# Scores of the last head pair moved from an insertion of their own into the one before it, in two attentions of a transformer kernel

## What is computed

```python
# first block: attention by blocks (block 256, so every query sees its own block, causally)
s_own = jnp.einsum('bhqd,bhld->bhql', qb, k_own).astype(jnp.float32) * scale
s_own = jnp.where(own_pos[None, :] <= q_pos[:, None], s_own, NEG_INF)
p = jax.nn.softmax(logits, axis=-1)
out = jnp.einsum('bhql,bhld->bhqd', p_own, v_own)

# second model, first layer: attention by picked keys (top 64 by an index score, causal)
logits = jnp.einsum('bqhd,bqkhd->bhqk', qb, k_sel).astype(jnp.float32) * (dh ** -0.5)
logits = jnp.where(valid[:, None], logits, -jnp.inf)
p = jax.nn.softmax(logits, axis=-1).astype(v.dtype)
out = jnp.einsum('bhqk,bqkhd->bqhd', p, v_sel)
...
```

## Time and profile before

| | |
|---|---|
| median of 3 runs | 1026.43 us (1026.31 to 1026.63) |
| the profiled execution | 1026.1 us |
| its span, first to last instruction | 1024.3 us |
| TensorE busy | 1014.1 us (99%) |
| VectorE, ScalarE, GpSimd busy | 666.5, 568.6, 78.8 us |
| mean granted TensorE clock | 0.999 of 2.4 GHz |
| first attention beside its projection | 88.5 to 114.3 us of the span |
| second attention beside its projection | 510.4 to 537.4 us |

### The profile page before, as it was taken

The page is one execution under the profiler, slowest core; times in us unless marked ns, Lnnn a source line. Parts: engine busy times, 40 slices in busy tenths (PEclk is TensorE's granted clock), DMA queues, the critical chain, the costliest instruction groups (busy, mean ns, idle before and its releaser), DMA issues.

```text
span 1024.3 us, 14335 instructions
## 1 busy us (share of the span) xinstructions
PE 1014.1 (99%) x5178; PEld 853.1 (83%) x5178; DVE 666.5 (65%) x1077; ACT 568.6 (56%) x923; POOL 78.8 (8%) x113
## 2 busy tenths in 40 slices
PE   9999999999999999999999999999999999999997
PEld 7887888888888888787888888888899888888886
DVE  5666575467646554869957776666669858666663
ACT  6567465436545454766565654545566657454541
POOL 1010010001000000300050200000050001000000
PEclk9999999999999999999999999999999999999999
DMA  9746236314545455363424565554256324655521
GB/s 345 308 169 240 83 123 227 123 53 174 205 171 210 171 206 183 137 267 124 187 102 164 185 220 194 201 188 153 86 198 191 124 83 173 240 202 184 185 82 42
DMA packets 28959, 176.81 MB, mean 173 GB/s; under 512 B 3264, under 2 KB 3888, under 8 KB 10480
## 3 DMA queue, kind: packets, MB, share of 16 engines
q1 hardware_dynamic: 26784, 170.08, 46.0%
q0 software_dynamic: 1456, 5.48, 1.5%
q10 hardware_dynamic: 672, 0.62, 0.4%
HBM read 174.62 MB, written 1.05 MB: 172 GB/s over the span
## 4 chain that ended last, share of the span: by engine, by line
PE 94%; ACT 2%; DVE 2%; issue 1%; DMA 0%; POOL 0%; DVEq 0%; ACTq 0%; POOLq 0%
PE PS L1883 68%; PE PS L2208 10%; PE PS L2212 5%; PE PS L1957 3%; PE PS L2060 1%; ACT w_hi L646 1%; PE PS L1997 1%; PE PS L2014 1%; ACT work L826 1%; PE PS L2038 1%; PE PS L2468 1%; PE PS L2562 1%; PE PS L2571 1%; PE PS L2140 0%; DMA work<-in_gains 0%
## 5 line engine op out<-in xcount | busy, mean ns | idle before, releaser
L1883 PE MATMUL PS<-w_hi,hT 128*128 128x512 f32 (+2 forms) x1296 | 323.2, 388 | 0.6 <-DVE hT L1253 0.4
L1231 DVE SCALAR_TENSOR_TENSOR w_lo<-w_raw,gcol,w_hi 128x512 fp32r<-128x512 f32 (+4 forms) x318 | 260.7, 878 | 92.8 <-ACT w_hi L646 91.2
L646 ACT ACTIVATE w_hi<-w_raw,gcol 128x512 fp32r<-128x512 f32 (+4 forms) x326 | 244.6, 818 | 94.5 <-PE PS L1883 65.2
L1883 PEld LDWEIGHTS PS<-w_hi,hT 128*128 128x128 f32 x1296 | 236.6, 188 | 48.2 <-issue 2.6
L1225 DVE TENSOR_TENSOR w_lo<-w_raw,w_hi 128x1024 fp32r<-128x1024 f32 x118 | 143.2, 1245 | 86.9 <-ACT w_hi L646 86.1
L646 ACT ACTIVATE w_hi<-w_raw 128x1024 fp32r<-128x1024 f32 x118 | 119.6, 1052 | 97.8 <-PE PS L1883 92.6
L1883 PE MATMUL PS<-w_lo,hT 128*128 128x512 f32 (+2 forms) x648 | 172.3, 384 | 0.1
L2208 PE MATMUL PS<-hT,w_hi 128*128 128x512 f32 x448 | 156.5, 398 | 0.0
L1883 PEld LDWEIGHTS PS<-w_lo,hT 128*128 128x128 f32 x648 | 120.4, 188 | 23.9 <-DVE w_lo L1231 0.5
L2212 PE MATMUL PS<-hT,w_lo 128*128 128x256 f32 x448 | 116.6, 281 | 0.0
L1883 PE MATMUL PS<-w_hi,gT_hi 128*128 128x512 f32 x408 | 114.7, 393 | 0.0
(11 more groups left out here) (207 smaller groups left out, 821.6 us busy)
## 6 DMA issues: line engine op xcount, KB each, us to landing
w_raw<-in_w SPq DMA_DIRECT2D x64, 1024.0 KB, 4.8
w_raw<-in_w_gu SPq DMA_DIRECT2D x22, 1024.0 KB, 4.8
w_raw<-in_w_in SPq DMA_DIRECT2D x11, 1024.0 KB, 9.1
w_raw<-in_w_dn SPq DMA_DIRECT2D x22, 512.0 KB, 4.4
w_raw<-in_w_mem_k SPq DMA_DIRECT2D x4, 1024.0 KB, 4.9
w_raw<-in_w_out SPq DMA_DIRECT2D x4, 1024.0 KB, 4.8
w_raw<-in_w_cq SPq DMA_DIRECT2D x4, 1024.0 KB, 4.8
w_raw<-in_w_mem_v SPq DMA_DIRECT2D x4, 1024.0 KB, 4.8
```

Of the source, the lines that this page charges most:

```text
L646: act.activation(high, source, ACT.Copy, scale=1.0 if col is None else gcol[:, col + TURNED * k:col + TURNED * k + 1])\
L1231: ins = dve.scalar_tensor_tensor(out=lo, in0=raw, scalar=gcol[:, col + TURNED * k:col + TURNED * k + 1], in1=hi, op0=ALU.mult, op1=ALU.sub ...
L1883: mm = pe.matmul(bank(t, j)[:, 0:width], rows[:, kc0 + k, tok], w[:, s, at:at + width], start=begin and i == 0, stop=end and i == 2)
```

## The change

In both attentions the scores of pair 3 move from ahead of block (1,3) to ahead of block (0,3), right behind the turns of pair 1 (`turns_and_scores`, which was there for pairs 0 and 2). ScalarE's exponentials of pair 3 move ahead of the copy of token tile 0's projection result out of PSUM (`evict(0, ...)`), and in the first attention ahead of the split of unit 2 too, which also goes behind that copy. On VectorE the maxima of pair 3 move ahead of the split of unit 2 in the first attention; in the second one VectorE's order stays as it was. No instruction is added or removed; GpSimd's and SyncE's orders are the same.

```diff
@@ ScalarE, first attention
             for pair in range(2):
                 exponentials(moba, pair + 1)
                 copy_odd(moba, pair)
+            exponentials(moba, 3)
+            evict(0, rows2(k_tok), mem_rows)
             split_to(n["used"] + 2)
-            evict(0, rows2(k_tok), mem_rows)
-            exponentials(moba, 3)
             evict(1, rows2(k_tok), mem_rows)
@@ ScalarE, second attention
+            exponentials(dsa, 3)
             evict(0, rows2(vg_tok), even_rows)
-            exponentials(dsa, 3)
             evict(1, rows2(vg_tok), even_rows)
@@ VectorE, first attention
             copy_even(moba, 1)
+            masked_maxima(moba, 3)
             split_to(n["used"] + 2)
-            masked_maxima(moba, 3)
             copy_even(moba, 2)
@@ TensorE, first attention
-                           (0, 3): lambda: paired_turns(moba, 1), (1, 3): lambda: paired_scores(moba, 3)})
+                           (0, 3): lambda: turns_and_scores(moba, 1, 3)})
@@ TensorE, second attention
-                                                                (0, 3): lambda: paired_turns(dsa, 1), (1, 3): lambda: paired_scores(dsa, 3)})
+                                                                (0, 3): lambda: turns_and_scores(dsa, 1, 3)})
```

## The result

The changed kernel takes 1028.52 us (median of 16 runs, 1027.98 to 1030.16), the kernel before in the same series 1026.70 us (16 runs, 1026.17 to 1027.54). The difference is +1.82 us, the ratio 1.002 with a 95% interval of 1.0013 to 1.0026. So the change makes the kernel slower. The median difference is 0.18%, just under the 0.2% line, and the interval reaches from 0.13% to 0.26%, so it doesn't tell on which side of that line the loss lies.

The account below looks back on a forecast made before the run. TensorE, busy for 99% of the span, was taken to bound the kernel. Savings of 0.04 and 0.03 us and a new wait of 2.09 summed to +2.02 on 1026.43, giving 1028.45 us; range 1027.2 to 1029.2.

Parts of the forecast that it names:

- The new wait: Second attention: moved scores of pair 3 wait for VectorE's maxima 2, so TensorE stands still for 2.09 us.
- The saving: One seam between matmul kinds goes on TensorE in each attention: 0.04 us gained in the first, 0.03 in the second.
- The estimate from the Trainium skill's fixed part of a single matmul: Both attentions: some 175 ns of issue and drain saved per place, a gain of 0.35 us where the rows give 0.07.
- What the move displaces: First attention: later result copy and split of unit 2 delay the copy of turns 2; 0.8 us left, costed at nothing.
- Why VectorE is late: Second attention: two split pieces ahead of maxima 2 take 2.22 and 3.01 us, median 1.22, seemingly held by GpSimd's instructions.
- The delay absent outside the profiler: Rival, second attention: without GpSimd's delay of VectorE there is no stall, 1026.4 us; chance 0.12 for absent or halved.
- the delay fall otherwise: Same rival, second attention: GpSimd's delay differs; with half of it 1027.1 to 1027.5 us; chance 0.12 for absent or halved.
- A stall in the first attention: Rival: split of unit 2 comes too late, turns 3 wait for the copy of turns 2; 1028.9 or 1030.1 us; chance 0.04.
- A fall of the clock in the stall: Rival: TensorE granted 1.2 instead of 2.4 GHz behind the second attention's stall, each block 2.72 us more, 1031; chance 0.01.
- within 0.2%: Whole kernel: outcome that the change can't be told from no change, a line of 2.05 us; chance 0.53.

Follow-up runs that it names:

- second_only: The second attention's part of the change alone, with the first attention as in the kernel before: 1028.65 us against 1026.56, ratio 1.0023.
- before_tap_less: The kernel before with the third tap of GpSimd's convolution left out, against the kernel before: 1026.51 us against 1026.51, ratio 0.9999.

## Why the prediction was right

**The new wait: +2.09 us.** Measured 2.11 us in the changed kernel's trace, and +2.09 us for the second attention's part alone. The end of maxima 2 was foreseen as unmoved by the change, and it is: turns 1 to the end of maxima 2 is 525.21 - 522.42 = 2.79 us before and 526.00 - 523.20 = 2.80 after.

**The saving: -0.07 us.** Too small to measure in the medians, and somewhat too large in the sum. Turns 1 to turns 2 of the first attention, forecast to fall from 7.22 to 7.18 us, take 7.22, 7.22 and 7.21 in the three traces with the old order (the kernel before, second_only, before_tap_less) and 7.19 or 7.20 in the six with the new one. That is 0.02 us for 0.04. In the second attention it is 7.21 before and 7.20 in both experiments without a stall, 0.01 us for 0.03. The estimate from the Trainium skill's fixed part of a single matmul (TensorE: Matmul & The Clock Gate, section Single matmul latency), 0.35 us for both places, isn't borne out as I applied it: the joint form drops one seam and gains nearly nothing. The weight load of the scores is idle for 0.35 us behind a block and for 0.17 behind the turns, but this difference of 0.18 us doesn't come back in the distance between the starts. Why it doesn't isn't settled.

**What the move displaces: 0.** Foreseen for the first attention: the copy of turns 2 ends 0.8 us ahead of turns 3. Measured, the copy starts at 110.31 and takes 0.55, turns 3 start at 111.75, so 0.89 us:

```profile
108.03 2.36 DVE L1225 TENSOR_TENSOR w_lo<-w_raw,w_hi 128x1024 fp32r<-128x1024 f32 x2 [3.85 <-ACT w_hi L646]
110.31 0.55 DVE L1433 COPY work<-PS 128x384 f32<-128x384 f32 x1
```

VectorE idles 3.85 us ahead of the split that ScalarE now makes later, and the cover holds.

**Why VectorE is late.** The forecast read from two rows that a piece of the split is held until the GpSimd instruction beside it is over. The Trainium skill (GPSIMD Engine Reference, section Key points) names the contention, but not, in that section, its form. The runs show the form here: without the two instructions the pieces take 1.2 us, without the last one 2.21 and 1.21. The forecast passed over an earlier meeting of the same two kinds of instruction in which no piece is held; it is told in the last section.

**The rivals.** The delay absent outside the profiler: refuted, since the timed runs without the tap and with it differ by 1.9 us in the changed kernel (1028.52 and 1026.61, in two series whose kernels before lie 0.14 us apart) and not at all in the kernel before. Nor did the delay fall otherwise: the two pieces together take 5.13 to 5.15 us in all five traces that have the whole convolution and this order on VectorE. A stall in the first attention: none. A fall of the clock in the stall: none; TensorE was granted its full 2.4 GHz behind the stall in the changed kernel's trace, and the block behind the stalled scores takes 529.76 - 526.91 = 2.85 us, where before the block behind them took 529.63 - 526.76 = 2.87:

```profile
526.91 2.11 PE L1883 MATMUL PS<-w_hi,hT 128*128 128x512 f32 x8
...
529.76 1.98 PE L1883 MATMUL PS<-w_hi,hT 128*128 128x512 f32 x8
...
526.00:533.00 7.00, 6.95 (x37) 5.60 (x38) 1.67 (x9) 4.67 (x17) 0.00 (x0) 1.00 0.34 140
```

The 1.00 in the last line is the clock granted from 526 to 533 us. This holds for the profiled execution. Of the 16 timed runs the two longest (1030.07 and 1030.16 us) have the lowest mean clock, 0.997; the kernel before has such runs too (1027.75 and 1027.55 at 0.997). No trace of one was kept, so what makes them long isn't shown. They don't move the median.

**The chances.** The measured +1.82 us is 0.18%, on the side of "within 0.2%" that had 0.53. Most of the distance to 2.02 lies in the medians: the kernel before moved from 1026.43 (3 runs) to 1026.70 (16 runs), by 0.27 us. That the loss fell on this side of the line is luck: the second attention's part alone, with the same stall, measured +2.09 us, on the other side. That the time itself is met to 0.07 us is luck too, since the median of the kernel before moves by more than that.

## What to carry to other kernels

When a step moves earlier on the engine that sets the time, subtract its new start from the end of what it waits for; the margin that the old place had (0.7 us here) says nothing of the new one. Look on the releasing engine for work that isn't part of the chain and stands ahead of it, and move that behind when the consumer moves forward: here one line of VectorE's order was worth the whole 2.1 us. Check the distance between two insertions in the trace before joining them; if the joint form already stands there, its saving can be read off to a few hundredths of a us (0.07 foreseen, some 0.03 measured).

## What the runs showed of the hardware

A VectorE instruction that reads two SBUF operands (the split, 128 by 1024, 1.22 us alone) was held until a GpSimd elementwise instruction on SBUF that was under way had ended. Each held piece ended 1.07 to 1.09 us behind the end of the GpSimd instruction, in the kernel before, in the changed one, with the last addition left out (520.53 and 521.60) and with the maxima first (522.90 and 523.99).

GpSimd loses time as well. Its last addition starts 0.08 us after a piece has got its turn, which then runs for 1.00 us more, and takes 2.85 us in the order of the change; it takes 2.00 us where VectorE had no split waiting at its start:

```profile
520.90 2.00 POOL L574 TENSOR_TENSOR arena<-arena 128x1016 f32<-128x1016 f32 x1
```

The two engines don't take turns strictly, though. At the start of the convolution both pieces of the split before take their usual time, though a GpSimd instruction has begun beside the first; in the changed kernel:

```profile
510.33 2.36 DVE L1225 TENSOR_TENSOR w_lo<-w_raw,w_hi 128x1024 fp32r<-128x1024 f32 x2
...
510.61 3.85 POOL L571 TENSOR_TENSOR arena<-arena,conv_w 128x1024 f32<-128x1024 f32 x1 [75.06 <-DVE arena L1271]
```

This meeting looks the same in all nine traces. GpSimd's instruction takes 3.85 us, where the like multiplication of 128 by 1020 takes 1.90, and ends some 1.8 us behind the second piece; so it seems that here GpSimd was the one that waited, for both pieces. Why the second piece isn't held, as it is nine us later, isn't shown. A reader who took the hold for a rule would have foretold a delay here, and there is none.

VectorE's maxima, with one operand in PSUM and one in SBUF, aren't held: their two lengths, 0.28 and 0.42 us, are the same to about 0.01 us beside GpSimd and when it is idle.

The first projection starts between 8.96 and 10.32 us in the nine traces. Each kernel was traced once, so how much of this belongs to a kernel isn't shown (the two without the third tap are the latest, at 10.31 and 10.32). The spread is more than half of the effect that was looked for; a difference of two profiled spans would have given 2.8 us for 2.1.
